# Layers of a two-block model: scans three steps ahead of attention, first tile turned at the end of the layer before, first weights in two loads

## What is computed

```python
def first_block(x, ...):
    for l in range(DEPTH):                                   # DEPTH = 2
        mix = hybrid_mixer(x, w_in[l], ...)
        x = layer_norm(DN_ALPHA * x + mix, ln1_g[l], ln1_b[l])
        x = layer_norm(DN_ALPHA * x + swiglu(x, ffn_w1[l], ffn_w3[l], ffn_w2[l]), ln2_g[l], ln2_b[l])
    return x

def hybrid_mixer(x, ...):
    z_sgu, z_ssm, q, k, v, gates = jnp.split(x @ w_in, splits, axis=-1)
    br_a = spatial_gating(jax.nn.gelu(z_sgu), ...)           # layer norm of v, 128x128 mixing, times u
    br_b = s5_branch(z_ssm, ...)
    br_c = moba_attention(q, k, v)                           # 256 tokens: plain causal softmax with slopes
    g = jax.nn.sigmoid(gates)                                # three gates of width 1024
    merged = g[:, :, 0] * (br_a @ w_a) + g[:, :, 1] * (br_b @ w_b) + g[:, :, 2] * (br_c @ w_c)
    return merged @ w_out

def s5_branch(u, ...):
    lam_bar = jnp.exp(lam * dt)
    b_bar = ((lam_bar - 1.0) / lam)[..., None] * b_mat
    bu = jnp.einsum('gph,bsgh->bsgp', b_bar, ug)
    h = associative_scan of h[s] = lam_bar * h[s-1] + bu[s]
    y = gelu(real(c_mat @ h) + d * u)
    return y * sigmoid(y @ glu_w + glu_b)
```

## Time and profile before

| | us |
|---|---|
| median of three runs (lowest, highest) | 2191.64 (2191.57, 2194.16) |
| the profiled execution | 2188.97 |
| its span in the profile | 2187.2 |

### The profile page before, as it was taken

One profiled execution on the slowest core, in us unless ns is written; L12 is line 12 of the kernel. 1 busy time (PEld: TensorE's weight loads), 2 busy tenths in 40 slices (PEclk: granted clock), 3 DMA queues, 4 the chain that ended last, 5 costly groups with the idle time before them and its releaser, 6 DMA issues.

```text
span 2187.2 us, 34182 instructions
## 1 busy us (share of the span) xinstructions
PE 2061.2 (94%) x13823; PEld 1387.8 (63%) x13823; DVE 847.5 (39%) x1551; ACT 469.6 (21%) x880; POOL 248.0 (11%) x233
## 2 busy tenths in 40 slices
PE   7988999999998999999889999999997999999996
PEld 5776868864676786886344565699985443444342
DVE  1288230001237822000238865645456333233324
ACT  2255200000325510000032125433333101110110
POOL 2367100000037700000000001100000000000000
PEclk9999999999999999999989999999997899999998
DMA  7422444442642254444452224400012899999993
GB/s 236 149 83 89 179 138 154 154 154 85 199 145 91 83 192 140 150 149 149 153 188 74 92 100 154 155 3 4 3 44 87 336 396 395 395 412 395 392 395 154
DMA packets 138672, 385.45 MB, mean 176 GB/s; under 512 B 16903, under 2 KB 64367, under 8 KB 127409
## 3 DMA queue, kind: packets, MB, share of 16 engines
q1 hardware_dynamic: 138545, 383.61, 47.2%
HBM read 382.54 MB, written 1.05 MB: 175 GB/s over the span
## 4 chain that ended last, share of the span: by engine, by line
PE 41%; DVE 5%; ACT 2%; issue 1%; DMA 1%; DVEq 0%; POOL 0%; ACTq 0%; POOLq 0%
PE psum L1243 9%; PE psum L2820 9%; PE psum L1990 8%; PE psum L2844 5%; PE psum L2755 3%; PE psum L1442 1%; PE psum L2406 1%; ACT arena L1600 1%; PE psum L2059 1%; DVE arena L3033 1%; DVE arena L2955 1%; PE psum L2832 1%; PE psum L2008 1%; DMA ring<-in_w_ada_dram 1%; PE psum L2773 0%
## 5 line engine op out<-in xcount | busy, mean ns | idle before, releaser
L364 PE MATMUL psum<-arena,ring 128*128 128x256 f32 x1728 | 389.4, 385 | 17.2 <-DVE arena L935 15.9
L364 PEld LDWEIGHTS psum<-arena,ring 128*128 128x128 f32 x1728 | 330.3, 192 | 73.5 <-issue 16.6
L573 PE MATMUL psum<-arena,ring 128*128 128x256 f32 (+1 forms) x1536 | 306.8, 361 | 3.2 <-ACT arena L624 3.2
L573 PEld LDWEIGHTS psum<-arena,ring 128*128 128x128 f32 x1536 | 270.5, 189 | 39.3 <-ACT arena L624 4.0
L1990 PE MATMUL psum<-arena 64*64 64x64 f32 (+1 forms) x4320 | 179.9, 237 | 4.6 <-issue 1.9
L624 ACT ACTIVATE arena<-psum 128x512 f32<-128x512 f32 (+2 forms) x116 | 62.9, 567 | 542.2 <-PE psum L573 264.0
L1990 PEld LDWEIGHTS psum<-arena 64*64 64x64 f32 x4320 | 171.6, 134 | 6.8 <-issue 3.1
L600 PE MATMUL psum<-ring,arena 128*128 128x512 f32 x352 | 151.4, 592 | 0.0
L1243 PE MATMUL psum<-arena,ring 128*128 128x512 f32 (+2 forms) x432 | 142.2, 489 | 0.0
L1013 DVE TENSOR_TENSOR arena<-arena,psum 128x512 f32<-128x512 f32 x22 | 15.2, 690 | 288.8 <-PE psum L573 288.8
L600 PEld LDWEIGHTS psum<-ring,arena 128*128 128x128 f32 x352 | 66.9, 190 | 83.3 <-issue 83.2
(11 more groups left out here) (416 smaller groups left out, 2573.3 us busy)
## 6 DMA issues: line engine op xcount, KB each, us to landing
ring<-in_w_in_dram SPq DMA_DIRECT2D x31, 2048.0 KB, 8.1
ring<-in_ffn_w_dram SPq DMA_DIRECT2D x46, 1024.0 KB, 6.5
arena<-in_ex_gate_dram SPq DMA_DIRECT2D x15, 2048.0 KB, 11.2
arena<-in_ex_up_dram SPq DMA_DIRECT2D x15, 2048.0 KB, 15.7
arena<-in_ex_down_dram SPq DMA_DIRECT2D x15, 2048.0 KB, 17.5
ring<-in_ex_gate_dram SPq DMA_DIRECT2D x14, 2048.0 KB, 10.5
ring<-in_ex_up_dram SPq DMA_DIRECT2D x14, 2048.0 KB, 15.0
ring<-in_ex_down_dram SPq DMA_DIRECT2D x14, 2048.0 KB, 7.7
```

The lines of the kernel that those rows point to most:

```text
L364: ins = pe.matmul(bank[:, j, :], w[:, kc, c * P:(c + 1) * P], moving[:, kc, :], start=kc == 0, stop=kc == k - 1)
L573: ins = pe.matmul(bank[:, j, tokens], both[:, i * DC + kc, j * P:(j + 1) * P], K.xT[:, kc, tokens], start=kc == 0, stop=kc == DC - 1)
```

## The change

Four things are changed, all in the layers.

1. **The scans run three steps ahead** (`AHEAD = 3`). Angles, rotation, inputs and scan of steps 0 to 2 run ahead of the loop over the heads; head n runs those of step n + 3 (n up to 4). Sine, cosine and turned states get three buffers, the angles two. TensorE makes the outputs of steps 2b and 2b + 1 with the even head 2b, behind the gate, values and output of attention. On ScalarE the rotation moves from behind the drains to directly behind the exponentials. On VectorE the output step moves ahead of the probabilities, and the norm of v ahead of the first scans.
2. **The first tile is turned ahead.** At the end of a layer TensorE transposes tile 0 of the next layer into two banks ahead of the last unit's four products for tile 1; the first layer's tile 0 is turned ahead of the loop over the layers. In the last layer the transposes are made all the same and used by nobody.
3. **Slots.** The empty entry of `layer_units` moves from the end to before `w2`. Units 0 to 3 of `w2` run for all banks, only 4 and 5 tile by tile.
4. **The first weights** of each layer (unit 1 of `w_in`) land as two loads of 1 MB with a semaphore each.

The core of the diff:

```diff
-    units += [("w2", c) for c in range(W2_UNITS)]
-    return units + [None] * (-len(units) % SLOTS)
+    units += [None] * (-(len(units) + W2_UNITS) % SLOTS)
+    return units + [("w2", c) for c in range(W2_UNITS)]
...
+    def states(n):
+        return [None] * (len(keys) % BANKS == BANKS - 1) + [("bu", n, c) for c in range(2)]
+
+    for n, key in enumerate((("q", 0), ("q", 1), ("k", 0))):
+        keys += [key]
+        keys += states(n)
+    keys += [("k", 1)] + [("av", i) for i in range(2)]
...
-        if n < 7:
-            keys += [None] * (len(keys) % BANKS == BANKS - 1) + [("bu", n + 1, c) for c in range(2)]
+        if n < HEADS - AHEAD:
+            keys += states(n + AHEAD)
         keys += [("gate", g) for g in GATES_WITH[n]]
         if n > 0:
             keys += [("pT", n - 1)]
-        if n % 2 == 1:
+        if n % 2 == 0:
+            keys += [("o", n // 2 - 1)] if n > 0 else []
             keys += [("y", n // 2)]
-        elif n > 0:
-            keys += [("o", n // 2 - 1)]
...
-    return keys
+    return keys + [("next", i) for i in range(2)]
...
-            sp.dma_start(K.slot_like(("w_in", c), weights), weights).then_inc(K.landed(("w_in", c)), 16)
+            to = K.slot_like(("w_in", c), weights)
+            if c == W_IN_ORDER[0]:
+                sp.dma_start(to[:, 0:DC // 2], weights[:, 0:DC // 2]).then_inc(K.sem["dma_first"], 16)
+                to, weights = to[:, DC // 2:], weights[:, DC // 2:]
+            sp.dma_start(to, weights).then_inc(K.landed(("w_in", c)), 16)
...
-            pe.wait_ge(K.landed(("w_in", unit)), K.landed_count(("w_in", unit), l))
+            first = unit == W_IN_ORDER[0] and 0 in tiles
+            if first:
+                pe.wait_ge(K.sem["dma_first"], K.count("dma_first", l))
+            else:
+                pe.wait_ge(K.landed(("w_in", unit)), K.landed_count(("w_in", unit), l))
             w = K.weights(("w_in", unit), DC, BANK)
             for tt in tiles:
                 pe.wait_ge(K.empty((name, tt)), K.empty_count((name, tt), l))
                 bank = K.bank((name, tt))
                 for kc in range(DC):
+                    if first and kc == DC // 2:
+                        pe.wait_ge(K.landed(("w_in", unit)), K.landed_count(("w_in", unit), l))
                     ins = pe.matmul(bank, K.xT[:, kc, tt * P:(tt + 1) * P], w[:, kc, :], start=kc == 0, stop=kc == DC - 1)
                 ins.then_inc(K.full((name, tt)), 1)
...
-        for tt in range(TT):
-            turn("x_in", "xT", tt)
-            turned("xT", tt)
-            tokens("v", 1, [tt])
+        tokens("v", 1, [0])
+        turn_tile("x_in", "xT", 1)
+        turned("xT", 1)
+        tokens("v", 1, [1])
...
         state_inputs(0)
-        project("k", 4)
+        project("q", 3, [1])
+        state_inputs(1)
+        project("k", 4, [0])
+        state_inputs(2)
+        project("k", 4, [1])
         tokens("av", 5)
...
                 attend_scores(n)
-            if n < 7:
-                state_inputs(n + 1)
+            if n < HEADS - AHEAD:
+                state_inputs(n + AHEAD)
             for g in GATES_WITH[n]:
                 gates(g)
             if n > 0:
                 attend_values(n - 1)
-            if n % 2 == 1:
+            if n % 2 == 0:
+                if n > 0:
+                    attend_out(n // 2 - 1)
                 state_outputs(n // 2)
-            elif n > 0:
-                attend_out(n // 2 - 1)
...
 
-        for u in range(W2_UNITS - SLOTS):
+        for u in range(W2_UNITS - 2):
             pe.wait_ge(K.landed(("w2", u)), K.landed_count(("w2", u), l))
             down(u, list(banks)).then_inc(K.used_up(("w2", u)), 1)
-        for tt in range(TT):
-            for u in range(W2_UNITS - SLOTS, W2_UNITS):
-                if tt == 0:
-                    pe.wait_ge(K.landed(("w2", u)), K.landed_count(("w2", u), l))
-                ins = down(u, [(tt, hf) for hf in range(2)])
-                if tt == 1 and u < W2_UNITS - 1:
-                    ins.then_inc(K.used_up(("w2", u)), 1)
+        for u in range(W2_UNITS - 2, W2_UNITS):
+            pe.wait_ge(K.landed(("w2", u)), K.landed_count(("w2", u), l))
+            down(u, [(0, hf) for hf in range(2)])
+        down(W2_UNITS - 2, [(1, hf) for hf in range(2)]).then_inc(K.used_up(("w2", W2_UNITS - 2)), 1)
+        for i in range(2):
+            pe.wait_ge(K.sem["x_in"], K.count("x_in", l, 2 * TT + i + 1))
+            pe.wait_ge(K.empty(("next", i)), K.empty_count(("next", i), l))
+            turn(("next", i), 0, i)
+        for hf in range(2):
+            down(W2_UNITS - 1, [(1, hf)])
+        for i in range(2):
+            pe.wait_ge(K.empty(("next", i)), K.drained_count(("next", i), l))
 
...
+        def rotation(n):
+
+            act.wait_ge(K.sem["angle"], K.count("angle", l, n + 1))
+            if n >= 3:
+                act.wait_ge(K.sem["h_ready"], K.count("h_ready", l, n - 2))
...
                                     bias=K.negmax[:, n % 2, 1:2], scale=HD ** -0.5,
                                     accum_out=K.rowsum[:, n % 2, 1:2]).then_inc(K.sem["exped"], 1)
+            if n < HEADS - AHEAD:
+                rotation(n + AHEAD)
             for g in GATES_WITH[n]:
                 drain(("gate", g), K.gates[:, 2 * g:2 * g + 2, :], ACT.Sigmoid, src=pairs)
             if n > 0:
                 turned(n - 1)
             if n > 0 and n % 2 == 0:
                 attended(n // 2 - 1)
...
+            if tt == 0:
+                for i in range(2):
+                    turned_half(("next", i), l, 0, i)
 
...
-            if n:
-                pool.wait_ge(K.sem["cos_sin"], K.count("cos_sin", l, n))
-            out = K.angle.rearrange("p (j t) -> p j t", j=2)
+            if n >= 2:
+                pool.wait_ge(K.sem["cos_sin"], K.count("cos_sin", l, n - 1))
...
+        for n in range(AHEAD):
+            angles(n)
         pool.wait_ge(K.sem["v_norm"], K.count("v_norm", l))
         for tt in range(TT):
             pool.tensor_tensor(K.v_ln[:, tt, :], K.v_ln[:, tt, :], K.v_gain, ALU.mult).then_inc(link.sem, 1)
...
-            if n < 6:
-                angles(n + 2)
+            if n < HEADS - AHEAD:
+                angles(n + AHEAD)
             turn_back(n)
...
             dve.wait_ge(K.sem["cos_sin"], K.count("cos_sin", l, n + 1))
-            c, s, t = K.cos[:, n % 2, :], K.sin[:, n % 2, :], K.dve_tmp
+            if n:
+                dve.wait_ge(K.sem["scanned"], K.count("scanned", l, n))
+            c, s, t = K.cos[:, n % 3, :], K.sin[:, n % 3, :], K.dve_tmp
...
             dve.wait_ge(link.sem, link.count())
             ts_op(K.negmax[:, b, :], K.negmax[:, b, :], -HD ** -0.5, None, ALU.mult).then_inc(K.sem["neg_max"], 1)
-            if n < 7:
-                scan(n + 1)
+            if n < HEADS - AHEAD:
+                scan(n + AHEAD)
+            if n % 2 == 1:
+
+                c = n // 2
+                dve.wait_ge(K.full(("y", c)), K.full_count(("y", c), l))
+                dve.scalar_tensor_tensor(out=K.zssm[:, c, :], in0=K.zssm[:, c, :], scalar=V[:, 96 + c:97 + c],
+                                                   in1=K.bank(("y", c))[:, 0:T], op0=ALU.mult, op1=ALU.add).then_inc(K.empty(("y", c)), 1)
             dve.wait_ge(K.sem["exped"], K.count("exped", l, n + 1))
             dve.reciprocal(K.rowsum[:, b, :], K.rowsum[:, b, :]).then_inc(link.sem, 1)
...
-            if n % 2 == 1:
-
-                c = n // 2
-                dve.wait_ge(K.full(("y", c)), K.full_count(("y", c), l))
-                dve.scalar_tensor_tensor(out=K.zssm[:, c, :], in0=K.zssm[:, c, :], scalar=V[:, 96 + c:97 + c],
-                                                   in1=K.bank(("y", c))[:, 0:T], op0=ALU.mult, op1=ALU.add).then_inc(K.empty(("y", c)), 1)
         pairs = lambda bank: bank.rearrange("p (k n) -> p k n", k=2)
```

109 lines of the change are left out of this document (59 added, 50 removed).

## The result

Ten runs of each: before 2190.18 us in the median (2188.19 to 2194.16), after 2197.84 us (2193.68 to 2203.03). The ratio is 1.0031, with a 95% interval of 1.0020 to 1.0042: slower by 0.3%, where -4.5 us was forecast. A ratio is worked out from all runs of both kernels and need not be the quotient of the two medians.

What follows compares the result with a forecast made beforehand. TensorE was taken as nearly always busy, stopped by VectorE's score step and a GpSimd-ScalarE-VectorE ring. Start -2.6, border -7.4, way out -6.5, loops and bbar +12.0 gave -4.5: 2187.1 us, own range 2181 to 2193.

Steps and rivals of the forecast that it cites:

- The loop over the heads: Attention heads: old waits vanish, TensorE waits 9.3 us before gate 1 and 9.5 before inputs 6; 5.3 us later per layer.
- The term of 5.3 us a layer: Loop over the heads: `branch(0)` starts at 237.5 instead of 232.26, so each layer is 5.3 us slower.
- the sum of 5.98 us: VectorE in each head: time from score step to the scan's first product, through exponentials, table load to last cosine, and semaphore.
- The border: Between the two layers: last product to second tile takes 10.0 us instead of 17.4, 7.4 us saved.
- TensorE then goes on at once: Between the two layers: after the last products TensorE starts the next tile without waiting, since weights were loaded two units earlier.
- Bbar: Six VectorE products before the heads: GpSimd's company hits one or two, +0.7 us per layer; upper bound 6.2 less 0.8 slack.
- The start: First weights of the kernel, landing as two loads: 2.6 us saved, 1.5 or 0 in worse cases.
- The way out: From the last layer into the second block: w_ada's unit 3 lands 5.5 us earlier; 6.5 us saved, bounds 3 and 8.
- That long waits cost more clock: Rival, loop over the heads: clock loss grows with the wait to 5.3 us, +12.3 us in all, 2199.4; chance 0.14.
- The rival that the scans don't meet GpSimd: Loop over the heads: a head takes 13.2 us, gate 1 waits 3.6, inputs 6 not at all; 2151.7, chance 0.14.
- wide 2178 to 2200: Total time: the range said to hold all but the rival of 2151.7 us and small tails.
- the fourth rival: Bbar, before the heads: all six products held up, 5.4 us per layer instead of 0.7, +9.4, 2196.5; chance 0.05.

Runs made afterwards that it cites:

- the quiet version: The changed kernel with GpSimd's work in the loop over the heads cut to 8 or 16 columns, order and semaphores kept: 2172.73 us, ratio 0.9927.
- the version with all four edits: The changed kernel with score steps paired, rotation ahead of exponentials, turned-tile wait behind the jump, angles and rotation 1 behind bbar work: 2146.78 us, ratio 0.9804.

## Why the prediction was wrong, point by point

- **The loop over the heads was right in its mechanism and near in its size.** Waits of 9.16 and 9.50 us for 9.3 and 9.5, VectorE's head of 18.80 for 18.85. The term of 5.3 us a layer measured 7.3 and 6.1. What was missing is small, in layer 0: 0.7 us of low clock at the first scores; 0.7 us over the three heads of VectorE, since from head 2 on the table load of the exponentials, 1.28 us, lies in the chain too, which the sum of 5.98 us did not have; and behind the second wait the low clock cost 3.0 us (2.08 for 1.13 and 16.15 for 14.13), not 2.24.
- **The border failed: -7.4 became -1.3.** The step that failed is "TensorE then goes on at once". It asked for tokens and weights and not for TensorE's own instructions, whose fetch the sum put at nothing and the new wait ahead of the jump put off. That was the largest error, 6.1 us: 4.49 us of standing and 1.7 us of low clock in the tile behind it. The saving was there (7.8 us once the wait stood behind the jump).
- **Bbar was mis-sized: 0.7 measured 3.4 and 2.5.** I took the lower end because of L898, which took 681 to 683 ns in all 16 cases, and the scan's row was not the only one that shows the clash. In the kernel before, L902, the product behind L898 and of the same form, had shown it too (min/median/max in ns):

```profile
L902 DVE TENSOR_TENSOR arena<-arena x16: 692/1486/1646, 81.7 to 750.8; 128x512 f32<-128x512 f32 x16
```

  The difference is what GpSimd does when the product starts. L898 always started beside GpSimd's rounding step (a TENSOR_SCALAR), beside nothing, or in the last 0.13 us of a TENSOR_TENSOR; in the 13 cases in which L902 took over 1 us a TENSOR_TENSOR was running. In the changed kernel L898's line (now L945) takes up to 1.51 us, beside a TENSOR_TENSOR. Of the six products of bbar the two that started beside a TENSOR_TENSOR took 1.80 and 1.42 us, those beside a TENSOR_SCALAR 0.69, 0.98 and 0.69. The Trainium skill's rule (SBUF — State Buffer, Who interferes with whom), by which a product with two SBUF inputs contends with a GpSimd instruction that reads SBUF, agrees with the trace beside a TENSOR_TENSOR. GpSimd's TENSOR_SCALAR reads SBUF too and mostly cost nothing here, so the rule gave too much (5.4 us) and my 0.7 too little.
- **The clock ahead of the heads was not in the sum.** 2.0 us in layer 0 and 0.4 in layer 1. In layer 0 products that wait for nothing ran at the low clock (L499 at 111.25 took 2.08 us for 1.16, at a granted clock of 0.50); why the clock fell there stays open. It varies between executions: the ten runs of after spread over 9 us, those of before over 6.
- **The start was right in most executions.** The second tile starts at 21.71 in the profile of after, at 19.9 to 20.3 in seven of the other profiles with two loads, at 21.0 to 21.2 in three (2.6 us less than 23.06 is 20.5). The old start varies as well: 24.15 in the other profile that has it.
- **The way out was right in its mechanism and near in size:** -7.4 for -6.5. One wait for w_ada is left, 2.98 us, where there were three.
- **The rivals.** That long waits cost more clock did not happen: 9.16 us of waiting lost 2.1 us, as 3.93 us had lost 2.2. The rival that the scans don't meet GpSimd did not happen, since the same semaphore does start both; the quiet version shows that its wait at gate 1 was right and its wait of nothing at the inputs of step 6 wrong, so that its gain of 35 us against the forecast was too large (25 us measured against the changed kernel).
- **The direction was wrong.** 2197.84 lies outside the forecast's own 2181 to 2193 and within the wide 2178 to 2200, but slower had only 0.19. It is near the fourth rival's 2196.5, and that is luck: bbar gave 4.5 us more than the forecast in both layers together, not 9.4, and the border, which no rival held, gave 6.1.

## What to carry to other kernels

Before a wait goes ahead of a loop's jump back, ask what TensorE's queue can no longer do: a wait there delays the fetch of what follows, and 4.5 us was its price here. When one buffer is held by the second half of a pair, look for the order in which both halves are consumed at once; it was worth 17 us on top of the deeper pipeline, which alone made the loop slower, and nothing without it. An instruction that was never slow in a trace has been shown immune only to what its neighbour was doing at those moments.

## What the runs showed of the hardware

- TensorE's instruction fetch shows only in the DMA view: a late fetch cost 1.6 us with empty rings, 4.5 us behind a 2 MB load and parameters. In the timeline it is a wait released by "issue".
- VectorE's scan pieces take 0.67 us alone and 1.63 to 1.69 beside GpSimd's products (TENSOR_TENSOR), whose own time rises from 1.27 to 1.53 us. Beside GpSimd's TENSOR_SCALAR a VectorE product with two SBUF inputs took 0.68 or 0.69 us (0.98 twice, when it started 0.4 us into it). With GpSimd's products cut to a few columns the scans are at 0.67 again.
- The clock's loss behind a wait did not follow the wait's length: 2.2 us behind 3.93, 2.1 behind 9.16, 3.0 behind 9.50, none behind the 1.97 us wait in layer 1 of the version with all four edits.
